# Up projections of three feed-forward stages: another order of wide and narrow products in each

## What is computed

```
def swiglu_ffn(x, norm_g, w_in, w_out):
    gate, up = jnp.split(rmsnorm(x, norm_g) @ w_in, 2, axis=-1)
    return (jax.nn.silu(gate) * up) @ w_out
...
        u = jax.nn.relu(rmsnorm_2(x, ln2[l]) @ w_ff1[l])
        x = x + (u * u) @ w_ff2[l]
```

## Time and profile before

| | |
|---|---|
| median of 3 runs | 1037.01 us (1036.83 to 1037.03) |
| the profiled execution's own time | 1036.92 us |
| its span, first to last instruction | 1035.2 us |
| mean granted clock of TensorE | 0.999 |
| TensorE busy (PE) | 1017.5 us, 98% |
| VectorE busy (DVE) | 714.2 us, 69% |
| ScalarE busy (ACT) | 540.3 us, 52% |

### The profile page before, as it was taken

The page is one execution under the profiler, slowest core; times in us unless marked ns, Lnnn a source line. Parts: engine busy times, 40 slices in busy tenths (PEclk is TensorE's granted clock), DMA queues, the critical chain, the costliest instruction groups (busy, mean ns, idle before and its releaser), DMA issues.

```text
span 1035.2 us, 15770 instructions
## 1 busy us (share of the span) xinstructions
PE 1017.5 (98%) x6374; PEld 872.3 (84%) x6374; DVE 714.2 (69%) x1123; ACT 540.3 (52%) x846; POOL 91.7 (9%) x143
## 2 busy tenths in 40 slices
PE   8998999999999999999999999999999999999997
PEld 8976888888889957888888889999779988888885
DVE  5998866666667696657766678748756457656654
ACT  6336545455454596555545553545655445444442
POOL 4000390000010131000000021000000000000000
PEclk9999999999999999999999999999999999999999
DMA  9983656666636404755766646554245345665631
GB/s 267 250 203 103 200 176 194 203 198 179 200 82 212 156 1 123 224 163 169 219 202 183 202 133 216 173 163 164 82 163 178 107 148 177 191 204 176 201 125 41
DMA packets 189327, 174.71 MB, mean 169 GB/s; under 512 B 13028, under 2 KB 164708, under 8 KB 189255
## 3 DMA queue, kind: packets, MB, share of 16 engines
q1 hardware_dynamic: 187280, 169.67, 54.2%
q10 hardware_dynamic: 1398, 3.12, 0.9%
q0 software_dynamic: 576, 0.92, 0.3%
HBM read 171.76 MB, written 1.93 MB: 168 GB/s over the span
## 4 chain that ended last, share of the span: by engine, by line
PE 88%; DVE 6%; ACT 4%; issue 1%; POOL 0%; DMA 0%; ACTq 0%; POOLq 0%; DVEq 0%
PE bank L1982 15%; PE bank L1984 15%; PE bank L1983 15%; PE bank L2050 11%; PE bank L2054 11%; PE bank L2053 5%; PE bank L2051 5%; DVE split_lo L1167 2%; PE bank L2234 2%; DVE xn L1184 1%; ACT xn L740 1%; PE bank L2434 1%; DVE v L1685 1%; PE bank L2006 1%; PE bank L2650 1%
## 5 line engine op out<-in xcount | busy, mean ns | idle before, releaser
L1167 DVE TENSOR_TENSOR split_lo<-raw,split_hi 128x2048 fp32r<-128x2048 f32 (+1 forms) x159 | 356.5, 2247 | 140.7 <-ACT split_hi L700 140.4
L700 ACT ACTIVATE split_hi<-raw 128x2048 fp32r<-128x2048 f32 (+1 forms) x159 | 297.5, 1874 | 88.7 <-PE bank L1984 82.2
L2050 PE MATMUL bank<-xn,split_hi 128*128 128x512 f32 x480 | 190.5, 397 | 0.7 <-DVE xn L1184 0.7
L2054 PE MATMUL bank<-xn,split_hi 128*128 128x512 f32 x480 | 189.9, 396 | 0.0
L1982 PE MATMUL bank<-xn,split_hi 128*128 128x256 f32 (+2 forms) x496 | 143.1, 289 | 2.3 <-DVE xn L1184 1.6
L1983 PE MATMUL bank<-xn,split_hi 128*128 128x256 f32 (+2 forms) x496 | 140.2, 283 | 0.0
L1984 PE MATMUL bank<-xn,split_lo 128*128 128x256 f32 (+2 forms) x496 | 140.1, 283 | 0.0
L2053 PE MATMUL bank<-xn,split_lo 128*128 128x256 f32 x480 | 133.6, 278 | 0.0
L2051 PE MATMUL bank<-xn,split_lo 128*128 128x256 f32 x480 | 133.2, 277 | 0.0
L1982 PE MATMUL bank<-split_hi,ffa_hi 128*128 128x512 f32 x320 | 124.9, 390 | 0.0
L1984 PE MATMUL bank<-split_hi,ffa_lo 128*128 128x512 f32 x320 | 124.5, 389 | 0.0
(11 more groups left out here) (344 smaller groups left out, 1342.2 us busy)
## 6 DMA issues: line engine op xcount, KB each, us to landing
raw<-in_ffn_w_in SPq DMA_DIRECT2D x88, 512.0 KB, 5.1
raw<-in_w_ff SPq DMA_DIRECT2D x32, 1024.0 KB, 5.5
raw<-in_ffn_w_out SPq DMA_DIRECT2D x22, 1024.0 KB, 5.0
raw<-in_w_in SPq DMA_DIRECT2D x14, 1024.0 KB, 5.2
raw<-in_w_xkv SPq DMA_DIRECT2D x8, 1024.0 KB, 5.4
raw<-in_a_pw_w SPq DMA_DIRECT2D x12, 512.0 KB, 7.3
raw<-in_a_pw_w SPq DMA_DIRECT2D x4, 1024.0 KB, 9.7
raw<-in_b_w_in SPq DMA_DIRECT2D x4, 1024.0 KB, 5.9
```

What stands on the lines that cost most here:

```text
L700: nc.scalar.activation(split_slot[m % SPLITS][0][:, 0:n], raw[c % RAWS][:, 0:n], ACT.Copy).then_inc(split_hi, 1)
L1167: return nc.vector.tensor_tensor(dst, src, hi.bitcast(F32), ALU.subtract)
L2050: mm(whole, hi, xn_both[:, :, kt, :], start=kt == 0, stop=False)
L2054: x = mm(whole, hi, xn_both[:, :, kt, :], start=False, stop=kt == KT - 1)
```

## The change

`both_halves` gets the order as a function. Four orders are written; with W for wide, N for narrow, and kt rising within each kind:

- `in_turn`: W N W N W N ..., both tiles of each pair of `ffn0_in`, and the pairs of `first_wide_pair` in all three stages;
- `wide_first`: 8 W, then 8 N, both tiles of each pair of `ffn1_in`;
- `in_twos`: W N N W W N N W ..., the order before; the first tile of each pair of `ff_in`;
- `from_second`: W N N W N W N W ..., the second tile of each pair of `ff_in`.

```
+            ORDERS = {"ffn0_in": (in_turn, in_turn), "ffn1_in": (wide_first, wide_first),
+                      "ff_in": (in_twos, from_second)}
+
+            def both_halves(b, w, c0, order, kts=range(KT), ready=None):
 
                 whole = bank[b][:, :].rearrange("p (e t) -> p e t", e=2)
-                for kt in kts:
+                steps = order(kts)
+                for n, (kt, wide) in enumerate(steps):
                     if ready is not None and kt % 2 == 0:
                         te.wait_ge(xn_ready, ready + kt // 2 + 1)
                     hi, lo = part(w, ALL, kt, slice(c0, c0 + P))
-                    if kt % 2 == 0:
...
+                    stop = kts[-1] == KT - 1 and n == len(steps) - 1
+                    if wide:
+                        x = mm(whole, hi, xn_both[:, :, kt, :], start=kt == 0, stop=stop)
                     else:
...
+                        x = mm(bank[b][:, 0:S], lo, xn[0][:, kt, :], start=False, stop=stop)
                 return x
...
-                both_halves(b, w, 0).then_inc(first_tile, 1)
-                used(c, both_halves(b + 1, w, P))
+                first, second = ORDERS[stage]
+                both_halves(b, w, 0, first).then_inc(first_tile, 1)
+                used(c, both_halves(b + 1, w, P, second))
```

More of the change, by code:

```diff
@@ L2040, in features, with in_turn, wide_first, in_twos @@
                 return x
-            def both_halves(b, w, c0, kts=range(KT), ready=None):
+            def in_turn(kts):
+                return [(kt, wide) for kt in kts for wide in (True, False)]
+            def wide_first(kts):
+                return [(kt, wide) for wide in (True, False) for kt in kts]
+            def in_twos(kts):
+                return [(kt, wide) for kt in kts for wide in ((True, False) if kt % 2 == 0 else (False, True))]
+            def from_second(kts):
+                return [(kt, wide) for kt in kts for wide in ((True, False) if kt == 0 else (False, True))]
+            ORDERS = {"ffn0_in": (in_turn, in_turn), "ffn1_in": (wide_first, wide_first),
+                      "ff_in": (in_twos, from_second)}
+            def both_halves(b, w, c0, order, kts=range(KT), ready=None):
                 whole = bank[b][:, :].rearrange("p (e t) -> p e t", e=2)
-                for kt in kts:
+                steps = order(kts)
+                for n, (kt, wide) in enumerate(steps):
                     if ready is not None and kt % 2 == 0:
@@ L2048, in both_halves @@
                     hi, lo = part(w, ALL, kt, slice(c0, c0 + P))
-                    if kt % 2 == 0:
-                        mm(whole, hi, xn_both[:, :, kt, :], start=kt == 0, stop=False)
-                        x = mm(bank[b][:, 0:S], lo, xn[0][:, kt, :], start=False, stop=False)
-                    else:
-                        mm(bank[b][:, 0:S], lo, xn[0][:, kt, :], start=False, stop=False)
-                        x = mm(whole, hi, xn_both[:, :, kt, :], start=False, stop=kt == KT - 1)
+                    stop = kts[-1] == KT - 1 and n == len(steps) - 1
+                    if wide:
+                        x = mm(whole, hi, xn_both[:, :, kt, :], start=kt == 0, stop=stop)
+                    else:
+                        x = mm(bank[b][:, 0:S], lo, xn[0][:, kt, :], start=False, stop=stop)
                 return x
@@ L2061, in wide_pair @@
                     te.wait_ge(*before)
-                both_halves(b, w, 0).then_inc(first_tile, 1)
-                used(c, both_halves(b + 1, w, P))
+                first, second = ORDERS[stage]
+                both_halves(b, w, 0, first).then_inc(first_tile, 1)
+                used(c, both_halves(b + 1, w, P, second))
             def first_wide_pair(k, stage):
                 c, w = weights(stage, 0, KT)
-                both_halves(0, w, 0, range(4), xn_before[k])
+                both_halves(0, w, 0, in_turn, range(4), xn_before[k])
                 turn_half(k, 1)
-                both_halves(1, w, P, range(4))
-                both_halves(0, w, 0, range(4, KT), xn_before[k]).then_inc(first_tile, 1)
-                used(c, both_halves(1, w, P, range(4, KT)))
+                both_halves(1, w, P, in_turn, range(4))
+                both_halves(0, w, 0, in_turn, range(4, KT), xn_before[k]).then_inc(first_tile, 1)
+                used(c, both_halves(1, w, P, in_turn, range(4, KT)))
             def tokens(dst, w, cols, t, k0=0, k1=KT, ready=None, left=None):
```

## The result

The changed kernel took **1040.22 us** (median of 7 runs, 1039.93 to 1040.9) beside 1037.01 for the kernel before in the same rounds (7 runs, 1036.7 to 1037.38): a ratio of **1.0029 [1.002, 1.0038]**, slower by 3.0 us by the ratio (3.2 by the medians). The forecast was 1037.4, with a range up to 1039.7. Rival A's time, 1040.3, came true; whether its reason did is what the experiments ask. The profiled execution took 1040.43 us.

The account below looks back on a forecast made before the run. TensorE was taken as the bound, through distances between product starts. First stage 0, second +0.4, last 0, first pairs and waits 0 sum to +0.4 us on 1037.01 (three-run median): 1037.4 us, range 1035.0 to 1039.7.

Parts of the forecast that it names:

- Rival A: First stage and partly last, in turn: each step between shapes takes its longer value, +2.3 and +0.6 us, 1040.3 us; chance 0.17.
- What bounds it: Three reordered stages: TensorE busy all the time at clock 1.00, nothing waits for another engine; only distances between starts count.
- First stage, 0, ends -2.7 and +2.3: First feed-forward stage, 42 tiles in turn: summed steps give 0.350 us a pair against 0.348, taken as no change.
- Second stage, +0.4: Second feed-forward stage, 42 tiles, eight wide then eight narrow: 1.84 + 0.96 us a tile, +0.4 us, ends -2.0 and +2.3.
- Last stage, 0, up to +0.6: Last stage, 15 pairs: only the second tile changes, 6 of 8 product pairs in turn; 0, ends -0.7 to +0.6 us.
- First pairs and doubled waits, 0 and 0: Three first pairs, 6 tiles in turn: 0 within 0.4 us; 12 more waits on xn_ready, already met: 0, at most 0.8.
- B: Second stage: narrow run bound by its own loads, 0.12 a step, wide steps stay 0.233; +1.6 us, 1038.6 us; chance 0.12.
- C: First and last stage: in turn pays the lower step values, 0.34 us a pair; -2.7 and -0.7 us, 1034.0 us; chance 0.10.
- D: Second stage: the wide run settles at once, 2.74 us a tile; -2.0 us, 1035.0 us; chance 0.08.
- The rule on weight loads: TensorE's queue: if several weight loads ran ahead, mixed orders would be best, narrow runs worst; rows showed only one ahead.

## Why the prediction was wrong, step by step

- **What bounds it: right.** TensorE full in all three windows at a clock of 1.00, other engines' busy times unmoved, no idle time at the stages or at the new waits. All that the three stages gained or lost is in the distances between starts, as the text said it would be. (Its windows start at the third tile pair and not at the second; no term hangs on that.)
- **First stage, 0, ends -2.7 and +2.3: the step that failed.** It measured +1.98, of which +1.5 is the tiles' own, at 0.3533 a pair and 2.822 a tile where 2.78 to 2.80 was to be seen; with the down projection's excess a tile is 2.838. "By the steps of the present order: 0.235 + 0.115 = 0.350 us for a pair" takes the step from one kind to the next for a price that the kind carries into another order. It isn't: a step from wide to narrow was 0.230 to 0.236 in the order in twos, 0.232, 0.236 and 0.241 in the dear pace, 0.230 to 0.234 in the cheap one. The argument for the middle ("each kind of step shows both of its values ..., which says that the next product's shape alone doesn't set them") was true and pointed the other way: if the shape doesn't set them, a sum over shapes can't give the new order's pace, and both ends stood equally open.
- **A term that was left out.** The down projection behind a stretch starts irregularly by how the stretch ended: 5.50, 5.47 and 5.46 us in the three stages, where the kernel before has 5.44. Over the 10, 10 and 14 of them that changed that is 0.6 + 0.2 + 0.2, some 1.0 us of the 3.0. The prediction has no term for it. The tiles alone, some +2.0 us in the three stages, would have stayed inside the range.
- **Second stage, +0.4: right in the number, in part by luck.** The steady tile was read rightly from another stage's stretch: 1.84 and 0.95 where 1.84 and 0.96 was read, 2.793 a tile. But the first tile of each four is 0.017 us cheaper than before, so that four tiles take 11.146 us against 11.143, and of the stage's +0.30 the tiles have 0.06 and the down projections, which the sum left out, 0.21.
- **Last stage, 0, up to +0.6: low.** +0.70: +0.42 from the second tile of each pair, 2.816 where it was 2.787, which is within the end, and +0.22 from the down projections. The middle failed with the first stage, from which it was taken.
- **First pairs and doubled waits, 0 and 0: right,** a ratio of 1.0 [0.9991, 1.001], and within 0.03 us a stage in the trace.
- **Rival A:** place and threshold were right, the time in part by luck: it has 2.3 and 0.6 us for the tiles of the first and last stage, which cost 1.5 and 0.4, and nothing for the down projections, which cost 1.0. Its reason, that changes between lengths cost, fell with 64 columns of weights, where in turn is cheapest, and with the second pace. **B:** in the second stage wide steps go from 0.233 or 0.236 down to 0.227 within each run, as forecast, not as B had it. **C** would be right for 64-column loads, exactly at its 0.34. **D** comes nearest in the first tile behind a down projection: 2.766 against its 2.74.
- **The rule on weight loads.** The Trainium skill (TensorE: Matmul & The Clock Gate, Part 2, the step on LDWEIGHTS) has loads pulled ahead of matmuls under way. In the up projections the rows after still show one load ahead and no more: the load labelled with the narrow product of 197.36 starts at 197.12, with the wide product before it (PEld in order of time, kernel after).

```profile
197.12 0.19 PEld L2073 LDWEIGHTS bank<-xn,split_lo 128*128 128x128 f32 x1
```

Had several loads run ahead there, as the prediction weighed, the orders that mix most should have been cheapest. With 128 columns in turn was dearest or cheapest by its start, so the order's price says nothing for or against it. Elsewhere in the kernel before, where loads have 32 columns of weights (L2234, 43.1 to 79.8 us), two to four loads have started ahead of their products, counted by their starts: the trace agrees with the rule there, and in the up projections, with loads of 128 columns, it shows one at a time.

Shown: mixed lengths are needed; each order settles into a steady pace; in turn has two, 0.3467 and 0.3533; behind a down projection the start of the stretch chooses, and the choice lasts. Not shown: what in TensorE makes these paces, why a start in turn leads into the dear one behind every down projection, what chooses behind a wait, where the same start went both ways, and which of the 19 good starts would serve with other loads. No run here separates TensorE's reading of columns from its writing to PSUM.

## What to carry to other kernels

Don't price a new order of products by adding up steps read in the old one. Measure a stretch of the new order from its first start to the end of the stage behind it, and look for its repeating group; if no such stretch exists, keep both ends of the range equally open. Where lengths are mixed, the first few products of a stretch can be worth more than the rest of the order: one kernel with a different start in every stretch measures them all in one run. Try the one chosen at every place, since it held behind like work and not behind a wait.

## What the runs showed of the hardware that was not expected

- Products of one length go at one pace: 0.2267 us with 512 columns, 0.120 with 256, with 128 columns of weights. Alternating 512 with 256 in turn goes at 0.3467 (their sum) or at 0.3533, and stays there for the 28 pairs to the end of the stretch.
- Less work in the loads can make an order slower: in twos went from 2.787 us a tile with 128 columns of weights to 2.800 with 64, while in turn went from 2.838 to 2.728.
- A stretch passes its irregularity on: up to 0.06 us in the first ten products of the down projection behind it, which are all alike.
